# Half of the SSM input moved from the first stage to a later chunk, with the vector engine's order and the slots of the side jobs moved to match

## The chip, the core and the metric

The kernel runs on one core of one Trainium2 chip. The metric is the time of one execution on the device in microseconds (us), the median of three runs. TensorE is called PE here, VectorE DVE, ScalarE ACT, GpSimd POOL and SyncE SP, as in the profile.

## The reference, cut to what matters

One layer over 256 tokens of width 2048, all in 32-bit floats:

```
mod  = silu(c) @ W_ada + b_ada                 # shift1, scale1, gate1, shift2, scale2, gate2
h    = rms_norm(x) * (1 + scale1) + shift1
p    = h @ W_in                                # conv value, conv gate, ssm input u, ssm gate: 1024 columns each
yc   = swish(layer_norm(causal_conv31(value * sigmoid(gate))))
ys   = gelu(diagonal_ssm(u) + u * d) * sigmoid(ssm_gate)
x    = x + gate1 * (concat(rms_norm(yc), rms_norm(ys)) @ W_out)
x    = x + gate2 * top2_of_32_experts(rms_norm(x) * (1 + scale2) + shift2)
out  = rms_norm(x)
```

The state-space model (SSM) is worked in eight quads of 128 channels: per quad PE makes the drive from one tile of u, DVE rotates it, scans it in two halves and rotates it back, and PE reads the states out into one tile of the SSM's output.

## The kernel before, in words

**Weights.** All large weights pass through `ring`, 12 buffers of 1 MB. SP starts one load per unit in a fixed order; the load of unit n waits until PE has consumed unit n - 12. There are 40 units in stage A, 88 in stage B, 16 in stage C (the output projection), and then 48 for each of eight rounds of four experts (L484).

**Stage A** (`A_LIST`, L67): for each quarter b of the 2048 channels, four units of the scale columns of W_ada, four of the shift columns, and, between the units of quarter b + 1, two units of W_in for u (all 1024 columns, two rows of channels each). A column unit is eight matmuls (L524). After four of them PE signals, ACT copies the row (`column_copy`, L1110), PE turns it into columns (`columns`, L535), DVE adds the bias, and after a shift DVE scales hT (L1566), on which the u units of that quarter wait (L563). In the same stage DVE makes the phases of the sine and cosine tables (L1595 to L1600) behind its `columns(3)`; ACT turns them into tables (L1148, L1153, L1157), and its `column_copy(4)` stands in its queue behind L1148, `column_copy(5)` behind L1153. The last u unit releases the eight tiles of u.

**Stage B** is 24 steps. Step g is 2 or 3 `ada` units (eight matmuls each, L707, for gate1, shift2, scale2 and gate2, 16 units a part, all into PSUM bank 2), `side(2g)`, one unit of a chunk of W_in (32 matmuls, L722; four units make a chunk of 512 columns), and `side(2g + 1)`. `CHUNKS` lists the chunks. The lists `DRIVE_AT`, `READ_AT` and `SUM_AT` put the side jobs into slots: the drive of a quad (L755), the read-out of a quad (L769, L772, then ACT's gelu, L1200), and three sums over channels (L740) for the conv's layer norm and RMS norm. PE runs its program in order, so a side job that is not ready stops it. Between two parts of the ada units stands a chain: PE's first unit of part i + 1 waits for ACT's `ada_copy(i)` (L1181, out of bank 2 into `modrow`), and `ada_copy(i)` waits until POOL's `columns(i - 1)` (L1387 to L1401) has emptied `modrow`. In before, the last units of the parts fall into steps 5, 11, 17 and 23.

**POOL** works, in its order: the skip diagonals of the quads (L1380, each behind the read-out of the quad before it), `columns(0)` to `columns(3)`, and the two products value * gate (`z_tiles`, L1410). Its order in before is diagonals 0 to 3, columns(0), diagonal 4, z_tiles(1), diagonal 5, columns(1), diagonal 6, z_tiles(0), diagonal 7, columns(2), columns(3).

**DVE** works quads 0 to 4, the upper half of the conv (`convolve(1, 0)`: 124 instructions, L1664 and L1668, back to back), quads 5 and 6, the lower half of the conv, the tile sum (L1677), then centring, the sum of squares, scaling, the first half of quad 7, the last sum of squares, `norm_conv` (L1697, L1699), and the second half of quad 7. The tables, the conv and other tiles share memory: conv lies on the cosines of quads 0 to 3.

**ACT**, in step 19, waits for scale2 (`parts_ready` 3) and stores scale2 and shift2 to memory, and in step 20 waits for that store and loads them back as rows; the copy of the first sum (L1205) stands behind this.

**Stage C**: output unit 0 waits for the last chunk and for `norm_conv`; then read-out 7, units 1 and 2, the SSM's sum of squares, and so on. Behind the 16 units come the router and the experts.

Of the kernel before, what the change touches and what calls it, by code (L numbers as in the profile page):

```python
# [61 lines left out]
A_UNITS, B_UNITS, C_UNITS, D_UNITS = 40, 88, 16, 48  # L62
# [17 lines left out]


def ada_in_step(g):

    return 3 if g % 3 else 2
# [6 lines left out]
DRIVE_AT = [0, 1, 4, 7, 10, 13, 27, 29]  # L91
READ_AT = [3, 7, 9, 13, 15, 29, 32, 49]
SUM_AT = [42, 44, 47]
# [18 lines left out]
def stored_before(chunk, b):  # L112

    return 2 + b if chunk == 0 else 4 + 2 * (chunk - 1) + b + 1
# [7 lines left out]
def trunk(nc, a, out):  # L122

    ctx = ExitStack()
    with ctx:
# [308 lines left out]
        def _(sp):  # L434
# [10 lines left out]
            for n, (kind, b, i) in enumerate(A_LIST):  # L445
                unit = ring[:, n % RING, :]
                if kind == "u":
                    k = 4 * b + 2 * i
                    start(n, unit.rearrange("p (k n) -> p k n", k=2), w_in[:, k:k + 2, 2 * CH:3 * CH])
# [54 lines left out]
        def _(pe):  # L504
# [46 lines left out]
            def u_unit(n, b, i):  # L551

                if b == 0 and i == 0:
# [4 lines left out]
                def tiles(pair, kk):  # L558
                    k = 4 * b + 2 * i + kk
                    pe.wait_ge(h_ready, k + 1)  # L560
                    for j in range(2):
                        o = kk * CH + (2 * pair + j) * P
# [4 lines left out]
                if b == 3 and i == 1:  # L567
                    for pair in range(4):
                        for kk in range(2):
                            last = tiles(pair, kk)  # L570
                        if pair < 3:
# [3 lines left out]
                else:  # L575
                    for kk in range(2):
                        for pair in range(4):
# [59 lines left out]
            def a_unit(n):  # L637
                kind, b, i = A_LIST[n]
                if kind == "u":
                    u_unit(n, b, i)  # L640
# [23 lines left out]
            for n in range(8, 14):  # L664
                a_unit(n)
            turn_blocks(0)
            turn_blocks(1)
            columns(2)
            a_unit(14)
            a_unit(15)  # L670
            turn_blocks(2)
            turn_blocks(3)
            a_unit(16)
            a_unit(17)
# [3 lines left out]
            for n in range(18, 21):  # L678
                a_unit(n)
            turn_blocks(6)  # L680
            for n in range(21, 24):
# [3 lines left out]
            for n in range(24, 28):  # L685
                a_unit(n)
            columns(5)
            for n in range(28, 34):
                a_unit(n)
            columns(6)  # L690
            for n in range(34, 38):
                a_unit(n)
            columns(7)
            a_unit(38)
            a_unit(39)
# [18 lines left out]
            def chunk_unit(n, it, u):  # L714

                s = arrived(n)
                for kk in range(4):
                    k = 4 * u + kk
                    for j in range(4):
                        if k == 0 and j % 2 == 0:  # L720
# [21 lines left out]
            def side(slot):  # L742
                for job, q in side_jobs(slot):
                    if job == "drive":

                        pe.wait_ge(chunk_stored, q // 2 + 1)
# [11 lines left out]
                    elif job == "read":  # L758
                        if q:
                            pe.wait_ge(side_stored, q)  # L760
                        else:
                            pe.wait_ge(chunk_stored, 4)
# [277 lines left out]
        def _(act):  # L1040
# [127 lines left out]
            for pair in range(4):  # L1168
# [14 lines left out]
            def keep_chunk(it):  # L1183

                act.wait_ge(chunk_done, 4 + it + 1)
                _c0, kind, tile = CHUNKS[it]
                func, dst = {"gate": (ACT.Sigmoid, zT[:, :, PAD:]), "value": (ACT.Copy, vals), "out_gate": (ACT.Sigmoid, sgT)}[kind]
# [32 lines left out]
            for g in range(STEPS_B):  # L1220
# [17 lines left out]
            side(49)  # L1238
# [115 lines left out]
        def _(pool):  # L1354
# [51 lines left out]
            def z_tiles(h):  # L1406

                pool.wait_ge(chunk_stored, 4 + 2 * (VALUE_0, VALUE_1)[h] + 2)
# [71 lines left out]
        def _(dve):  # L1480
# [127 lines left out]
            def quad(q, middle=None):  # L1608
# [36 lines left out]
                if middle:  # L1645
                    middle()

# [326 lines left out]
```

## Time and profile before

| what | value |
|---|---|
| median of three runs | 1560.77 us (1560.55 to 1563.14) |
| the profiled execution's own time | 1561.5 us |
| its span | 1559.8 us |
| mean granted PE clock | 0.975 |
| busy share of the span, PE / DVE / ACT / POOL | 92% / 33% / 10% / 8% |
| end of the first stage's last u unit | 147.2 us |
| start of output unit 0 | 438.0 us |

Times in the profile are us from the span's start. A timeline row merges like instructions that follow one another: start, time from the first start to the last end, engine, line, operation, tiles, count, and in brackets the engine's idle time before the row and what ended it.

### The profile page before, as it was taken

To read this page: it belongs to the slowest core of one execution; us is meant where nothing else is said; L and a number is where in the kernel's file an instruction comes from. 1 tells how busy PE (TensorE), PEld (TensorE's weight loads), DVE (VectorE), ACT (ScalarE), POOL (GpSimd) and SP (SyncE) were. 2 spreads that over 40 slices of the span, in tenths; PEclk is the share of its full clock that TensorE was granted. 3 is DMA by queue.
4 is the path that set the end of the run, shared out by engine and by line. 5 is a ranking of instruction groups with operands and counts; after the bars stand their busy time and mean duration, and the time that the engine had idled before them with its cause. 6 is when DMAs were issued, how large, how long until landed. Compare 5 with 4: busy or idle time off the path is not lost.

```text
span 1559.8 us, 18926 instructions
## 1 busy us (share of the span) xinstructions
PE 1440.0 (92%) x7448; PEld 665.8 (43%) x7448; DVE 519.8 (33%) x934; ACT 160.0 (10%) x254; POOL 131.0 (8%) x112
## 2 busy tenths in 40 slices
PE   5999999989779979999999999999999999999967
PEld 2667666656534434343343343343343343343322
DVE  4231999999651230121121121111111111111105
ACT  3040100100310211010010010010010010000001
POOL 1000011539000017000000000000000000000000
PEclk9799999999989989999999999999999999999989
DMA  9999988979646437999999999999999999999991
GB/s 319 388 391 409 356 307 311 389 284 389 219 168 236 145 126 289 422 421 421 421 422 422 421 423 422 422 422 422 422 421 422 421 423 421 423 421 422 422 420 75
DMA packets 108961, 565.47 MB, mean 363 GB/s; under 512 B 10632, under 2 KB 10816, under 8 KB 50608
## 3 DMA queue, kind: packets, MB, share of 16 engines
q1 hardware_dynamic: 105984, 559.98, 89.2%
q10 hardware_dynamic: 2928, 4.81, 1.0%
q8 instruction: 34, 0.56, 0.1%
q14 instruction: 15, 0.12, 0.0%
HBM read 562.62 MB, written 2.13 MB: 362 GB/s over the span
## 4 chain that ended last, share of the span: by engine, by line
PE 62%; DVE 13%; DMA 11%; issue 7%; PEld 4%; PEldq 1%; SPq 1%; ACT 1%; POOL 0%; DVEq 0%; ACTq 0%
PE ps L918 20%; PE ps L952 15%; DMA ring<-in_exp_w_down 10%; PE ps L890 7%; PE ps L972 6%; PE ps L722 3%; DVE arena L1668 3%; PE ps L563 3%; DVE arena L1635 2%; PEld ps L811 2%; PE ps L508 2%; DMA ring<-in_w_ada 1%; PE ps L707 1%; PE ps L524 1%; DVE arena L1623 1%
## 5 line engine op out<-in xcount | busy, mean ns | idle before, releaser
L918 PE MATMUL ps<-ring,arena 128*64 128x512 f32 x2048 | 458.4, 594 | 11.3 <-DMA ring<-in_exp_w_up 7.7
L918 PEld LDWEIGHTS ps<-ring,arena 128*64 128x64 f32 x2048 | 154.6, 137 | 287.9 <-issue 285.9
L952 PE MATMUL ps<-ring,arena 128*64 128x512 f32 x1024 | 242.9, 600 | 26.8 <-issue 13.9
L722 PE MATMUL ps<-arena,ring 128*128 128x256 f32 x768 | 174.5, 386 | 0.4
L722 PEld LDWEIGHTS ps<-arena,ring 128*128 128x128 f32 x768 | 146.0, 192 | 36.8 <-issue 17.2
L952 PEld LDWEIGHTS ps<-ring,arena 128*64 128x64 f32 x1024 | 72.2, 137 | 167.0 <-issue 158.7
L1875 DVE TENSOR_TENSOR arena<-arena,ps 128x512 f32<-128x512 f32 x72 | 49.6, 689 | 277.5 <-PE ps L972 262.8
L890 PE MATMUL ps<-arena 128*64 128x256 f32 x1024 | 123.7, 386 | 6.4 <-issue 3.8
L811 PE MATMUL ps<-ring,arena 128*128 128x512 f32 x256 | 114.1, 605 | 5.8 <-DVE arena L1699 5.7
L1849 DVE TENSOR_SCALAR arena<-ps,mod 128x256 f32<-128x256 f32 x64 | 34.8, 544 | 228.4 <-PE ps L890 228.4
L972 PE MATMUL ps<-arena 128*64 128x512 f32 x448 | 106.5, 595 | 2.9 <-issue 1.9
L890 PEld LDWEIGHTS ps<-arena 128*64 128x64 f32 x1024 | 73.2, 138 | 69.9 <-issue 42.1
L1668 DVE SCALAR_TENSOR_TENSOR arena<-arena 128x256 f32<-128x256 f32 x240 | 95.2, 480 | 0.0
L811 PEld LDWEIGHTS ps<-ring,arena 128*128 128x128 f32 x256 | 49.0, 194 | 67.2 <-issue 66.9
L1863 DVE TENSOR_TENSOR arena<-arena,ps 128x512 f32<-128x512 f32 x16 | 11.0, 688 | 178.2 <-PEq L924 177.0
L1380 POOL TENSOR_SCALAR skip<-ident,vT 128x128 f32<-128x128 f32 x8 | 50.9, 6361 | 215.4 <-PE ps L772 212.9
L1856 DVE TENSOR_TENSOR arena<-ps,arena 128x512 f32<-128x512 f32 x64 | 44.3, 692 | 66.4 <-PEq L958 66.4
L1302 ACT ACTIVATE arena<-ps,mod 128x256 f32<-128x256 f32 x64 | 36.1, 564 | 279.0 <-PE ps L890 279.0
L972 PEld LDWEIGHTS ps<-arena 128*64 128x64 f32 x448 | 32.0, 137 | 70.1 <-issue 70.1
L707 PE MATMUL ps<-ring,ccol 128*32 128x512 f32 x512 | 59.8, 596 | 0.7 <-issue 0.5
L563 PE MATMUL ps<-arena,ring 128*128 128x256 f32 x256 | 57.0, 381 | 1.7 <-issue 0.9
L524 PE MATMUL ps<-ring,ccol 128*32 128x512 f32 x256 | 39.0, 729 | 18.8 <-DMA ring<-in_w_ada 18.8
(262 smaller groups left out, 747.1 us busy)
## 6 DMA issues: line engine op xcount, KB each, us to landing
ring<-in_exp_w_gate SPq DMA_DIRECT2D x128, 1024.0 KB, 19.7
ring<-in_exp_w_up SPq DMA_DIRECT2D x128, 1024.0 KB, 18.7
ring<-in_exp_w_down SPq DMA_DIRECT2D x128, 1024.0 KB, 22.5
ring<-in_w_ada SPq DMA_DIRECT2D x96, 1024.0 KB, 9.0
ring<-in_w_in SPq DMA_DIRECT2D x32, 1024.0 KB, 11.9
ring<-in_w_out SPq DMA_DIRECT2D x16, 1024.0 KB, 11.6
arena<-in_x SPq DMA_DIRECT2D x2, 1024.0 KB, 7.0
arena<-in_x SPq DMA_DIRECT2D x1, 2048.0 KB, 10.4
```

Of the source, the lines that this page charges most:

```text
L524: last = mm(ps[32 * j:32 * j + 32, bank, :], ccol[:, k:k + 1].to_broadcast([P, 32]), ring[:, s, j * N:(j + 1) * N], start=(i == 0), stop=( ...
L563: last = mm(ps[:, U_BANKS[pair], j * T:(j + 1) * T], ring[:, s, o:o + P], hT[:, k, :], start=(k == 0 and j == 0), stop=(k == KD - 1), skip ...
L707: last = mm(ps[32 * j:32 * j + 32, 2, :], ccol[:, k:k + 1].to_broadcast([P, 32]), ring[:, s, j * N:(j + 1) * N], start=(k == 0), stop=(k = ...
L722: last = mm(ps[:, j // 2, (j % 2) * T:(j % 2 + 1) * T], ring[:, s, kk * N + j * P:kk * N + (j + 1) * P], hT[:, k, :], start=(k == 0 and j ...
L811: last = mm(ps[:, OUT_BANKS[c][t], :], src[:, k0 + kk, t * P:(t + 1) * P], ring[:, s, kk * N:(kk + 1) * N], start=first, stop=end, skip_gr ...
L890: last = mm(ps[half, 6 + k % 2, 0:T], x1p[:, t, k, half], pick[:, t, :], start=(t == 0), stop=(t == 1), skip_group_check=True)
L918: last = mm(ps[64 * x:64 * x + 64, stage, :], xT[:, k, slot:slot + SLOTS], ring[:, s, kk * N:(kk + 1) * N], start=(k == 0), stop=(k == KD ...
L952: last = mm(ps[half, 2 + n, :], hidT[pr][:, u, half], ring[:, (m + x) % RING, n * N:(n + 1) * N], start=(u == 0), stop=(u == 3), skip_grou ...
L972: last = mm(ps[64 * x:64 * x + 64, 6 + t, :], wpickT[:, pr, t * P + 64 * x:t * P + 64 * x + 64], yexp[pr][:, n, :], start=(pr == 0), stop= ...
L1380: gp_.tensor_scalar(skip[:, :], ident[:, :], vT[:, 4, q:q + 1], None, ALU.mult).then_inc(skip_ready, 1)
L1668: ins = V.scalar_tensor_tensor(conv[:, c, :], z, cwT[:, c, j:j + 1], conv[:, c, :], ALU.mult, ALU.add)
L1875: V.tensor_tensor(acc[:, t, cc], acc[:, t, cc], ps[:, bank, :], ALU.add).then_inc(added, 1)
```

## The change

Half of u (512 of its 1024 columns, quads 0 to 3) stays in stage A, in four units of four rows of channels each; the other half becomes the third chunk of stage B. Stage A has 36 units, stage B 92 in 28 steps, with one ada unit in even and two in odd steps up to step 19, and then 4, 4, 4, 4, 4, 5, 5, 4. Only the first tile pair (two banks) of u is released at the end of stage A. DVE's order becomes quads 0 to 3, upper conv, quads 4 to 6, lower conv, the whole of the conv's norm, quad 7. POOL's z_tiles(1) stands ahead of diagonal 4 and columns(0), and z_tiles(0) ahead of columns(1). The store and reload of scale2 and shift2 move from ACT to SP, before stage C's units 8 and 9.

```diff
-A_UNITS, B_UNITS, C_UNITS, D_UNITS = 40, 88, 16, 48
+A_UNITS, B_UNITS, C_UNITS, D_UNITS = 36, 92, 16, 48
 for _b in range(3):
-    A_LIST += [("scale", _b + 1, 0), ("scale", _b + 1, 1), ("u", _b, 0), ("scale", _b + 1, 2), ("scale", _b + 1, 3),
-               ("u", _b, 1)] + [("shift", _b + 1, i) for i in range(4)]
-A_LIST += [("u", 3, 0), ("u", 3, 1)]
+    A_LIST += [("scale", _b + 1, 0), ("scale", _b + 1, 1), ("u", _b, 0), ("scale", _b + 1, 2), ("scale", _b + 1, 3)]
+    A_LIST += [("shift", _b + 1, i) for i in range(4)]
+A_LIST += [("u", 3, 0)]
-U_BANKS = [2, 0, 1, 3]
+U_BANKS = [2, 3]
-CHUNKS = [(1536, "gate", 4), (512, "value", 0), (1024, "gate", 0), (0, "value", 0), (3072, "out_gate", 0), (3584, "out_gate", 4)]
-VALUE_1, VALUE_0 = 1, 3
+CHUNKS = [(1536, "gate", 4), (512, "value", 0), (2560, "u", 4), (1024, "gate", 0), (0, "value", 0),
+          (3072, "out_gate", 0), (3584, "out_gate", 4)]
+VALUE_1, U_1, VALUE_0 = 1, 2, 4
-STEPS_B = 24
+STEPS_B = 28
 def ada_in_step(g):
-    return 3 if g % 3 else 2
+    if g < 20:
+        return 2 if g % 2 else 1
+    return 5 if g in (25, 26) else 4
-DRIVE_AT = [0, 1, 4, 7, 10, 13, 27, 29]
-READ_AT = [3, 7, 9, 13, 15, 29, 32, 49]
-SUM_AT = [42, 44, 47]
+DRIVE_AT = [0, 3, 6, 9, 25, 28, 31, 35]
+READ_AT = [5, 9, 13, 17, 31, 35, 38, 58]
+SUM_AT = [49, 51, 54]
...
                     sp.wait_ge(side_done, QUADS)
                     sp.dma_start(x1, a["x"][0].rearrange("(t p) d -> p t d", p=P)).then_inc(x_again, 16)
+                    sp.wait_ge(parts_ready, 3)
+                    for i, part in enumerate((4, 3)):
+                        sp.dma_start(col(ab_dram[i]), mod[:, part, :]).then_inc(ab_stored, 16)
+                if m == 9:
+                    sp.wait_ge(ab_stored, 32)
+                    sp.wait_ge(z_ready, 2)
+                    sp.dma_start(ab_rows, ab_dram.rearrange("i (k p) -> (i k) p", p=P)).then_inc(ab_landed, 16)
...
             out_units([0])
-            side(49)
             out_units([1, 2])
+            side(58)
+            out_units([3, 4])
             channel_sum(3)
-            out_units([3, 4])
+            out_units([5, 6, 7])
             pe.wait_ge(ab_landed, 16)
             tr(ps[:, 6, 0:2 * KD], ab_rows, 2 * KD).then_inc(ab_turned, 1)
-            out_units(range(5, 10))
+            out_units([8, 9])
...
-                if g == 9:
+                if g == 14:
                     act.wait_ge(parts_ready, 1)
                     act.dma_start(col(gate_dram[0]), mod[:, 2, :]).then_inc(gate_stored, 16)
-                if g == 19:
-                    act.wait_ge(parts_ready, 3)
-                    for i, part in enumerate((4, 3)):
-                        act.dma_start(col(ab_dram[i]), mod[:, part, :]).then_inc(ab_stored, 16)
-                if g == 20:
-                    act.wait_ge(ab_stored, 32)
-                    act.wait_ge(z_ready, 2)
-                    act.dma_start(ab_rows, ab_dram.rearrange("i (k p) -> (i k) p", p=P)).then_inc(ab_landed, 16)
...
             for q in range(4):
                 diagonal(q)
+            z_tiles(1)
+            diagonal(4)
             columns(0)
-            diagonal(4)
-            z_tiles(1)
             diagonal(5)
-            columns(1)
             diagonal(6)
+            diagonal(7)
             z_tiles(0)
             pool.wait_ge(z_ready, 2)
             gp_.memset(mean_w, 1.0 / CH).then_inc(sum_consts, 1)
-            diagonal(7)
+            columns(1)
             columns(2)
             columns(3)
...
-            for q in range(5):
+            for q in range(4):
                 quad(q)
             convolve(1, 0)
-            quad(5)
-            quad(6)
+            for q in range(4, 7):
+                quad(q)
             convolve(0, 1)
...
             scale_conv()
-
-            def finish_conv():
-                add_squares(2)
-                norm_conv()
-
-            quad(7, finish_conv)
+            add_squares(2)
+            norm_conv()
+            quad(7)
```

## Rows read from the trace of the kernel before

**Rows 1.** Windows of two stretches; columns: us, PE, PEld, DVE, ACT, POOL busy, PEclk, DMA share, GB/s

```profile
40.00:60.00 20.00, 19.71 (x111) 12.80 (x111) 7.88 (x15) 0.59 (x1) 0.00 (x0) 0.65 1.06 387
...
1000.00:1100.00 100.00, 96.18 (x502) 36.51 (x500) 15.92 (x25) 5.70 (x10) 0.00 (x0) 1.00 1.01 422
```

**Rows 2.** Timeline of PE in stage A

```profile
33.49 1.93 PE L524 MATMUL ps<-ring,ccol 128*32 128x512 f32 x8 [0.44 <-DMA ring<-in_w_ada]
...
101.43 0.95 PE L535 MATMUL ps<-arena,modrow 128*128 128x1 f32 x8
...
125.95 0.95 PE L535 MATMUL ps<-arena,modrow 128*128 128x1 f32 x8
...
133.14 14.05 PE L563 MATMUL ps<-arena,ring 128*128 128x256 f32 x64 [0.87 <-DVE arena L1566]
```

**Rows 3.** Timeline of DVE and ACT in stage A, the tables

```profile
83.58 4.42 DVE L1595 TENSOR_TENSOR arena<-arena 128x4096 f32<-128x4096 f32 x1
...
95.48 3.62 ACT L1148 ACTIVATE arena<-arena 128x4096 f32<-128x4096 f32 x1 [1.51 <-DVE rot L1600]
...
99.24 0.59 ACT L1110 COPY modrow<-ps 128x512 f32<-128x512 f32 x1
```

**Rows 4.** Timeline of PE in stage B, quiet steps

```profile
251.45 7.17 PE L722 MATMUL ps<-arena,ring 128*128 128x256 f32 x32
...
299.34 7.17 PE L722 MATMUL ps<-arena,ring 128*128 128x256 f32 x32
...
306.45 1.15 PE L755 MATMUL ps<-arena 32*128 32x256 f32 x16
...
307.52 2.78 PE L707 MATMUL ps<-ring,ccol 128*32 128x512 f32 x24
...
317.77 1.93 PE L772 MATMUL ps<-arena 128*32 128x256 f32 x32
```

**Rows 5.** Timeline of DVE: conv halves, starts of quads 5 and 6, tile sum

```profile
249.84 47.59 DVE L1668 SCALAR_TENSOR_TENSOR arena<-arena 128x256 f32<-128x256 f32 x120
...
297.35 2.28 DVE L1622 TENSOR_TENSOR arena<-ps,arena 128x2048 f32<-128x2048 f32 x1
...
316.16 2.29 DVE L1622 TENSOR_TENSOR arena<-ps,arena 128x2048 f32<-128x2048 f32 x1
...
338.15 47.60 DVE L1668 SCALAR_TENSOR_TENSOR arena<-arena 128x256 f32<-128x256 f32 x120
...
385.85 3.79 DVE L1677 TENSOR_REDUCE arena<-arena 128x256 f32<-128x2048 f32 x1
```

**Rows 6.** Timeline of POOL in stage B

```profile
280.89 17.46 POOL L1387 TENSOR_TENSOR modrow<-modrow,own 128x512 f32<-128x512 f32 x1 [31.16 <-ACT modrow L1181]
...
332.28 2.39 POOL L1410 TENSOR_TENSOR arena<-arena 128x1024 f32<-128x1024 f32 x1 [11.84 <-ACT arena L1194]
...
341.23 45.00 POOL L1380 TENSOR_SCALAR skip<-ident,vT 128x128 f32<-128x128 f32 x1 [6.29 <-PE ps L772]
...
386.19 1.06 POOL L1387 TENSOR_TENSOR modrow<-modrow,own 128x512 f32<-128x512 f32 x1
...
389.71 0.22 POOL L1396 TENSOR_TENSOR mod<-mod,bada 128x16 f32<-128x16 f32 x1
```

**Rows 7.** Timeline of PE around the end of stage B

```profile
406.15 1.19 PE L740 MATMUL ps<-arena 128*128 128x256 f32 x2 [6.12 <-issue]
...
407.14 9.62 PE L722 MATMUL ps<-arena,ring 128*128 128x256 f32 x32
...
437.99 9.59 PE L811 MATMUL ps<-ring,arena 128*128 128x512 f32 x16 [5.73 <-DVE arena L1699]
```

**Rows 8.** Timeline of ACT and SP, the first sum, the swish, the experts' second loads

```profile
397.79 0.37 ACT L1205 COPY arena<-ps 128x256 f32<-128x256 f32 x1 [19.65 <-DMA scale_shift_scratch<-mod]
...
412.00 4.04 ACT L1215 ACTIVATE arena<-arena,vT 128x256 f32<-128x256 f32 x8 [2.85 <-DVE arena L1693]
...
536.34 63.53 SPq L484 DMA_DIRECT2D ring<-in_exp_w_up  x8
```

More of the change, by code:

```diff
@@ L112, in stored_before @@
 def stored_before(chunk, b):
-    return 2 + b if chunk == 0 else 4 + 2 * (chunk - 1) + b + 1
+    return 2 + 2 * (chunk - 1) + b + 1 if chunk else 0
 JOB_ORDER = [(stage, pr, u, x) for pr in range(2) for stage in range(2) for u in range(4) for x in range(2)] + \
@@ L447, in _ @@
                 if kind == "u":
-                    k = 4 * b + 2 * i
-                    start(n, unit.rearrange("p (k n) -> p k n", k=2), w_in[:, k:k + 2, 2 * CH:3 * CH])
+                    start(n, unit.rearrange("p (k n) -> p k n", k=4), w_in[:, 4 * b:4 * b + 4, 2 * CH:2 * CH + N])
                 else:
@@ L548, in turn_x, with u_unit @@
                 last.then_inc(x_turned, 1)
-            def u_unit(n, b, i):
-                if b == 0 and i == 0:
+            def u_unit(n, b):
+                if b == 0:
                     pe.wait_ge(x_even, 4)
@@ L558, in tiles @@
                 def tiles(pair, kk):
-                    k = 4 * b + 2 * i + kk
+                    k = 4 * b + kk
                     pe.wait_ge(h_ready, k + 1)
                     for j in range(2):
-                        o = kk * CH + (2 * pair + j) * P
+                        o = kk * N + (2 * pair + j) * P
                         last = mm(ps[:, U_BANKS[pair], j * T:(j + 1) * T], ring[:, s, o:o + P], hT[:, k, :],
@@ L565, in tiles @@
                     return last
-                if b == 3 and i == 1:
-                    for pair in range(4):
-                        for kk in range(2):
+                if b == 3:
+                    for pair in range(2):
+                        for kk in range(4):
                             last = tiles(pair, kk)
-                        if pair < 3:
+                        if pair == 0:
                             last.then_inc(chunk_done, 1)
@@ L575, in u_unit @@
                 else:
-                    for kk in range(2):
-                        for pair in range(4):
+                    for kk in range(4):
+                        for pair in range(2):
                             last = tiles(pair, kk)
@@ L639, in a_unit @@
                 if kind == "u":
-                    u_unit(n, b, i)
+                    u_unit(n, b)
                 else:
@@ L663, in _ @@
             columns(1)
-            for n in range(8, 14):
+            for n in range(8, 13):
                 a_unit(n)
@@ L668, in _ @@
             columns(2)
+            a_unit(13)
             a_unit(14)
-            a_unit(15)
             turn_blocks(2)
             turn_blocks(3)
+            a_unit(15)
             a_unit(16)
-            a_unit(17)
             turn_blocks(4)
@@ L677, in _ @@
             turn_blocks(5)
-            for n in range(18, 21):
+            for n in range(17, 20):
                 a_unit(n)
             turn_blocks(6)
-            for n in range(21, 24):
+            for n in range(20, 22):
                 a_unit(n)
@@ L684, in _ @@
             columns(4)
-            for n in range(24, 28):
+            for n in range(22, 26):
                 a_unit(n)
             columns(5)
-            for n in range(28, 34):
+            for n in range(26, 31):
                 a_unit(n)
             columns(6)
-            for n in range(34, 38):
+            for n in range(31, 35):
                 a_unit(n)
             columns(7)
-            a_unit(38)
-            a_unit(39)
+            a_unit(35)
             def ada_unit(n, i, k):
@@ L719, in chunk_unit @@
                     for j in range(4):
-                        if k == 0 and j % 2 == 0:
+                        if it and k == 0 and j % 2 == 0:
                             pe.wait_ge(chunk_stored, stored_before(it, j // 2))
@@ L744, in side @@
                     if job == "drive":
-                        pe.wait_ge(chunk_stored, q // 2 + 1)
+                        pe.wait_ge(chunk_stored, q // 2 + 1 if q < 4 else 2 + 2 * U_1 + q // 2 - 1)
                         if q:
@@ L761, in side @@
                         else:
-                            pe.wait_ge(chunk_stored, 4)
+                            pe.wait_ge(chunk_stored, 2)
                         if sums_before(slot):
@@ L1167, in _ @@
             column_copy(7)
-            for pair in range(4):
+            for pair in range(2):
                 act.wait_ge(chunk_done, pair + 1)
@@ L1183, in keep_chunk @@
             def keep_chunk(it):
-                act.wait_ge(chunk_done, 4 + it + 1)
+                act.wait_ge(chunk_done, 2 + it + 1)
                 _c0, kind, tile = CHUNKS[it]
-                func, dst = {"gate": (ACT.Sigmoid, zT[:, :, PAD:]), "value": (ACT.Copy, vals), "out_gate": (ACT.Sigmoid, sgT)}[kind]
+                func, dst = {"u": (ACT.Copy, uT), "gate": (ACT.Sigmoid, zT[:, :, PAD:]), "value": (ACT.Copy, vals), "out_gate": (ACT.Sigmoid, sgT)}[kind]
                 if it == VALUE_0:
@@ L1406, in z_tiles @@
             def z_tiles(h):
-                pool.wait_ge(chunk_stored, 4 + 2 * (VALUE_0, VALUE_1)[h] + 2)
+                pool.wait_ge(chunk_stored, 2 + 2 * (VALUE_0, VALUE_1)[h] + 2)
                 z = zT[:, 4 * h:4 * h + 4, PAD:]
@@ L1607, in _, with quad @@
             dve.wait_ge(tables_ready, 2)
-            def quad(q, middle=None):
+            def quad(q):
                 b = q % 2
```

4 lines of the change are left out of this document (1 added, 3 removed).

## The prediction

> **What bounds the kernel now.** I read the windows first. In the expert rounds DMA is busy all the time at 422 GB/s [rows 1], and the last ring loads ahead of them are only released by the first expert matmuls [rows 8]. So the rounds end a fixed time after they begin, and they begin a fixed time after output unit 0, behind which PE has its queue full. What the change moves is the start of output unit 0, 438.0 in the trace [rows 7]. Then the timelines. Stage A is two lines at once: DMA is full (share 1.06, 387 GB/s, so 2.71 us for a unit of 1.049 MB [rows 1]) and yet PE waits for no load after 33.5 us [rows 2], since its own work is slower than the loads. It ends with the u units at 147.2 [rows 2]. Stage B is PE-bound while DVE runs beside it. At its end DVE comes last: PE waits 6.1 us for the second sum, whose chunk then takes 9.6 us where a warm one takes 7.2, and 5.7 us for the conv's norm, whose unit 0 takes 9.6 [rows 4, 7].
>
> An effect of less than 0.2% (3.1 us) can't be told from none here.
>
> **Stage A.** Four u units leave. Two take 14.05 us [rows 2], so PE has 28.1 us less to do. Not all of it comes off:
> - The tables. Two of the four stood ahead of `columns(4)`, so PE comes to it at 101.4 - 14.1 = 87.3. ACT's copy for it ended at 99.83 [rows 3], behind the sine and DVE's phases, which start behind `columns(3)` (83.58), with one u unit fewer ahead: 99.8 - 7.0 = 92.8. PE now waits 5.5 us where it waited for nothing.
> - The clock. After 6.1 us without work the next chunk took 2.5 us longer [rows 7, 4]; I take 2.5 us for this wait.
> - `columns(6)` was covered by a u unit ahead of it (125.95 [rows 2]); now the copy (0.59 [rows 3]) and two hand-overs show: 0.8 us.
> - DMA. The last u unit is number 35; unit 5 landed at 33.5 [rows 2], so it lands at 33.5 + 30 x 2.71 = 114.8, ahead of its use at about 120. No cost, with 5 us of cover.
> Stage B thus starts at 147.2 - 28.1 + 5.5 + 2.5 + 0.8 = 127.9.
>
> **Stage B, PE's work.** From 251.45 to 299.34 PE did five steps with 13 ada units [rows 4]. An ada unit is 2.78 / 3 less the overlap, 0.905; so a chunk unit with its hand-overs is (47.9 - 11.8) / 5 = 7.22. A drive is 1.07 (306.45 to 307.52), a read-out 2.4 (0.5 and 1.93 [rows 4]). After the change: 28 x 7.22 = 202.2, 64 x 0.905 = 57.9, 8 drives 8.6, 7 read-outs 16.8, three sums 1.5: 287.0 us.
>
> **The new waits.** Drive 5 waits until DVE has read drive 4, which is behind the upper conv: the value chunk ends with step 7, 80 us into the stage, and 1.1 us of copies, 3 of POOL, 49 of conv and 4.6 of reading (two instructions of 2.28 [rows 5]) follow, while PE comes to drive 5 after 135 us: 3 us. Read-out 6 and the first ada unit of part 2: 0.4 and 0.8 us.
>
> The large one is at step 24. Twice a POOL instruction that met the conv was held to its end: the product of `columns(1)` started at 280.89 and ended at 298.35, where alone it takes 1.06; diagonal 7 lasted from 341.23 to 386.23 [rows 5, 6]. Before, neither mattered. Now `columns(1)` stands directly behind z_tiles(0), whose end is what starts the lower conv. Its first instruction may slip in; the rest waits for the conv's end. ACT's copy of part 2 needs it, and part 3's first ada unit, the third of step 24, needs the copy. With t the end of step 19's chunk: copies 1.1, product 2.4, hand-overs 0.3, conv 48.9 [rows 5, 6] give t + 52.7; POOL's remaining 2.7 of its 3.7 us (386.19 to 389.93) and the copy make it t + 56.1. PE gets there after four chunks, 18 ada units and the 0.8: t + 46.0. PE stands still for 10.1 us, and then pays 2.5 for the clock.
>
> The Trainium skill (SBUF — State Buffer, Who interferes with whom) says that a DVE instruction with two SBUF inputs and a GpSimd instruction that reads SBUF exclude each other, the lock being held for one instruction. The trace agrees on the exclusion and not on the length: a conv instruction lasts 0.4 us, and POOL waited 45.
>
> **DVE after the lower conv.** Its end is t + 52.7, the tile sum 3.8 [rows 5] more; the first sum's slot is behind step 24's chunk, at t + 56.1 + 1.8 + 7.2 = t + 65.1. So PE is late by 8.6 us. From there DVE and ACT need 9 us to the second sum (8.4 from 397.79 to 406.15, and the first copy [rows 7, 8]) against PE's 11.8 (five ada units and a chunk); then 15 us to the third (4.7 from the second sum's end at 407.3 to the swish at 412.0, swish 4.0 [rows 7, 8], square 1.8, half of the 4096-column activation's 3.62 [rows 3], tile sum 3.8 [rows 5], hand-overs) against 15.3; then 5.7 for the norm [rows 7] against 7.2 of the last chunk and 1.3 for its copies, which PE does wait for. PE is the bound with little to spare, and ACT's wait for the reload of scale2, which held the first sum's copy (19.65 us idle behind it [rows 8]), is gone from the path. It moves to SP, ahead of C's units 8 and 9: issued with read-out 7, needed 35 us later; nothing. Quad 7 (18.8 us, 297.35 to 316.16 [rows 5]) runs behind the norm, beside output units 0 to 2; its read-out comes 21 us after unit 0's start. Nothing. The order of the SSM's tail behind units 3 and 4 has 7 us of cover (unit 5).
>
> DMA in steps 20 to 27: 42 units in about 100 us at 2.5 to 2.7 us each, 105 to 113, of which twelve (30 us) are in the ring at the start. No cost; if the ring were empty, 10 us.
>
> **The sum.** Output unit 0 starts at 127.9 + 287.0 + 3 + 0.4 + 0.8 + 10.1 + 2.5 + 1.3 = 433.0, which is 5.0 before 438.0; and it starts after 1.3 us of idleness, not 5.7, so that its 2.6 us for the clock go too. 7.6 us off the profiled execution's 1561.5 is 1553.9, and that execution stands 0.7 above the median: 1553.
>
> Bounds of the unseen costs: the clock's price after the two new waits, from 0 to 5 us each; the wait for `columns(1)`, from 0 (POOL gets in between conv instructions) to 12 (the first instruction is held too); the 3 us of drive 5, from 0 to 5.
>
> **The rivals.**
> 1. POOL isn't held. By the skill's rule as it stands, the lock ends with each 0.4 us instruction, `columns(1)` would be done some 10 us after its start, long before step 24. Worked out from rows: the 10.1, the 2.5 and their knock-on go, 0.7 for the first sum comes, and the end is 12 us earlier: 1541. Against it are two rows of 17 and 45 us that end exactly with a conv. 0.12.
> 2. DVE's chain misses its slots. The cover at the three sums is 8.6, 3 and 0.3 us. If scans or sums run longer, as beside POOL's work they can, PE waits at the third sum, goes cold and pays as before: 4 + 2.5 us, 1560. 0.10.
> 3. Slower: PE's clock falls in stage A and stays low. At 40 to 60 us the granted clock was 0.65 of full, and eight matmuls took 1.93 us at such a time where eight in stage B take 0.93 [rows 1, 2, 4]. With two u units fewer ahead of them, the column units 22 to 35 meet four waits in a row. All fourteen at the low clock cost 14 less the 2.5 counted, the two u units 2.5 each: 16.5 us, B starts at 144, and the end is 1553 + 16.5 = 1569. It decides from a B start at about 136 on (no gain) and 139 (slower). For it: the waits are new. Against: from 80 us on the trace has small waits and a full clock. 0.08.
> The forecast itself: 0.70.
>
> **Numbers.** The forecast's own range is 1548 to 1558. The range given takes in most of rival 2 and some of rival 1: 1543 to 1561; what is left out is most of rival 1 and rival 3, 0.18. Faster than 1557.7: 0.69 of the forecast and rival 1, with a little of rival 2, 0.82. Same: the rest of rival 2 and a little of rival 3, 0.09. Slower: 0.09.
>
> **What would show it.** Stage B's first matmul near 128; a wait of 5 us before `columns(4)`; POOL's second or third instruction of `columns(1)` lasting some 47 us and ending with the lower conv; PE idle 10 us in step 24 behind ACT's copy; the first sum without a wait; output unit 0 near 433 at 7 us; equal times from there on. The prediction is wrong if the B start is past 133, if `columns(1)` ends before the conv, or if PE waits for sums 2 or 3.

## The result, and the profile after

The changed kernel takes 1542.93 us (1540.21 to 1544.64, four runs) against 1560.66 (1559.72 to 1563.14, four runs of the kernel before on the same chip); the ratio is 0.9882, 95% interval 0.9863 to 0.9902. It is 17.7 us faster. The forecast was 7.8 us (1553, with a range of 1543 to 1561), so the sign was right and the size too small by more than half; the measured median lies at the lower edge of the range, 0.1 us outside it. The profiled execution took 1544.6 us, its span is 1542.9; before they were 1561.5 and 1559.8.

The first fence is the timeline of PE in the changed kernel, at the places where the prediction had a term. `columns` is now L544, a column unit L533, an ada unit L715, a chunk unit L730, the sums L748, the output units L819.

```profile
93.20 1.86 PE L544 MATMUL ps<-arena,modrow 128*128 128x1 f32 x8 [5.37 <-ACT modrow L1119]
...
94.99 5.42 PE L533 MATMUL ps<-ring,ccol 128*32 128x512 f32 x32
...
101.17 1.05 PE L544 MATMUL ps<-arena,modrow 128*128 128x1 f32 x8 [0.76 <-ACT modrow L1119]
...
113.79 1.05 PE L544 MATMUL ps<-arena,modrow 128*128 128x1 f32 x8 [0.75 <-ACT modrow L1119]
...
121.08 7.14 PE L572 MATMUL ps<-arena,ring 128*128 128x256 f32 x32 [0.86 <-DVE arena L1567]
...
128.48 1.06 PE L715 MATMUL ps<-ring,ccol 128*32 128x512 f32 x8 [0.26 <-issue]
...
264.97 1.15 PE L763 MATMUL ps<-arena 32*128 32x256 f32 x16 [1.14 <-DVE arena L1624]
...
316.84 0.67 PE L777 MATMUL ps<-arena,skip 128*128 128x256 f32 x2 [0.41 <-issue]
...
329.26 1.92 PE L715 MATMUL ps<-ring,ccol 128*32 128x512 f32 x16 [0.75 <-ACT modrow L1190]
...
373.08 1.92 PE L715 MATMUL ps<-ring,ccol 128*32 128x512 f32 x16 [0.75 <-ACT modrow L1190]
...
384.35 0.67 PE L748 MATMUL ps<-arena 128*128 128x256 f32 x2 [2.23 <-issue]
...
384.94 6.19 PE L715 MATMUL ps<-ring,ccol 128*32 128x512 f32 x40
...
423.02 20.84 PE L819 MATMUL ps<-ring,arena 128*128 128x512 f32 x48 [1.27 <-ACT arena L1203]
```

These answer to [rows 2, 4, 7]. `columns(4)` waits 5.4 us and then takes 1.86 instead of 0.95, the four units behind it 5.4 instead of 3.6: the granted clock between 93 and 101 us was 0.65, and 1.00 in the same work before (101 to 106 us). Stage B starts at 128.5 (147.4 before). Drive 5 waits 1.1 us, read-out 6 0.4, the first ada unit of part 2 0.75. Then the row that matters: the first ada unit of part 3, at 373.08, waits 0.75 us and not 10.1. PE therefore comes to the first sum too early and waits 2.2 us there, after which five ada units take 6.2 us instead of 4.5, at a granted clock of 0.76 (384 to 391 us). Output unit 0 starts at 423.0 (438.0 before), 1.3 us behind the last chunk, and three output units take 20.8 us.

The timelines of POOL and DVE around the lower conv (L1411 is the product, L1388 to L1397 `columns(1)`, L1662 and L1666 the conv) answer to [rows 5, 6]:

```profile
218.58 42.19 POOL L1381 TENSOR_SCALAR skip<-ident,vT 128x128 f32<-128x128 f32 x1 [7.28 <-PE ps L780]
...
327.73 2.18 POOL L1411 TENSOR_TENSOR arena<-arena 128x1024 f32<-128x1024 f32 x1 [7.63 <-ACT arena L1203]
...
330.14 1.21 POOL L1388 TENSOR_TENSOR modrow<-modrow,own 128x512 f32<-128x512 f32 x1
...
331.43 2.05 POOL L1391 TENSOR_TENSOR modrow<-modrow 128x256 f32<-128x256 f32 x4
...
333.92 0.32 POOL L1397 TENSOR_TENSOR mod<-mod,bada 128x16 f32<-128x16 f32 x1
...
373.11 8.29 POOL L1388 TENSOR_TENSOR modrow<-modrow,own 128x512 f32<-128x512 f32 x1 [38.88 <-ACT modrow L1190]
```

```profile
330.02 2.82 DVE L1662 TENSOR_SCALAR arena<-arena 128x256 f32<-128x256 f32 x4 [13.28 <-POOL arena L1411]
...
332.76 47.73 DVE L1666 SCALAR_TENSOR_TENSOR arena<-arena 128x256 f32<-128x256 f32 x120
...
380.59 3.66 DVE L1675 TENSOR_REDUCE arena<-arena 128x256 f32<-128x2048 f32 x1
```

A conv half is four tensor_scalar instructions and then 120 scalar_tensor_tensor instructions that overlap: each waits for the one four before it, starts 0.396 us after its predecessor and lasts 0.48. `columns(1)` came directly behind POOL's own work, 0.12 us after the first tensor_scalar, and was over at 334.2, 46 us before the conv's end. It wasn't held: its seven instructions took 4.1 us in all, against 3.7 in [rows 6]. DVE paid too, with 2.82 us for the four tensor_scalar instructions instead of the 1.38 to 1.46 that they take where `columns(1)` isn't beside them. Three of the seven POOL instructions began among the four tensor_scalar ones; the other four, all of at most 64 columns, among the first overlapping ones. But diagonal 4, which met the upper conv 5.9 us after its scalar_tensor_tensor instructions had begun, lasted 42 us, and the first instruction of `columns(2)`, at 373.11, lasted 8.3 us, past the end of the lower conv at 380.5.

Behind output unit 0 the times are nearly the same: the first expert matmul (L927) starts at 570.95, 17.2 us earlier than its counterpart of before at 588.13, where output unit 0 was 15.0 earlier and 2.6 us of slow clock in it are gone (9.6 us for 16 matmuls before, 20.8 for 48 now). The span is 16.9 shorter.

### The profile page after: what moved, and what is told of

It reads as the page before. It is cut to its first block, busy times and chain, and to the rows that moved or that the text cites. A ratio compares the mean times of both kernels' runs of the same rounds, so it can differ in the third digit from the quotient of the medians.

```text
span 1542.9 us, 18923 instructions
## 1 busy us (share of the span) xinstructions
PE 1440.0 (93%) x7448; PEld 663.8 (43%) x7448; DVE 516.6 (33%) x934; ACT 159.7 (10%) x254; POOL 116.3 (8%) x112
## 3 DMA queue, kind: packets, MB, share of 16 engines
q1 hardware_dynamic: 108368, 560.02, 90.4%
## 4 chain that ended last, share of the span: by engine, by line
PE 55%; DVE 12%; DMA 12%; PEld 8%; issue 8%; PEldq 3%; SPq 1%; ACT 1%; POOL 0%; DVEq 0%; ACTq 0%
PE ps L927 20%; PE ps L961 15%; DMA ring<-in_exp_w_down 10%; PE ps L899 8%; PE ps L981 6%; DVE arena L1666 6%; PEld ps L730 4%; PEld ps L819 2%; PE ps L517 2%; DMA ring<-in_w_ada 1%; PE ps L819 1%; DVE arena L1636 1%; PEldq L823 1%; PEldq L735 1%; PE ps L533 1%
## 5 line engine op out<-in xcount | busy, mean ns | idle before, releaser
L927 PE MATMUL ps<-ring,arena 128*64 128x512 f32 x2048 | 458.3, 594 | 11.7 <-DMA ring<-in_exp_w_up 8.1
L927 PEld LDWEIGHTS ps<-ring,arena 128*64 128x64 f32 x2048 | 154.7, 137 | 288.0 <-issue 286.2
L730 PE MATMUL ps<-arena,ring 128*128 128x256 f32 x896 | 200.8, 383 | 0.1
L730 PEld LDWEIGHTS ps<-arena,ring 128*128 128x128 f32 x896 | 168.4, 190 | 42.2 <-issue 20.9
L819 PE MATMUL ps<-ring,arena 128*128 128x512 f32 x256 | 111.4, 594 | 1.3 <-ACT arena L1203 1.3
L1666 DVE SCALAR_TENSOR_TENSOR arena<-arena 128x256 f32<-128x256 f32 x240 | 95.3, 480 | 0.0
L819 PEld LDWEIGHTS ps<-ring,arena 128*128 128x128 f32 x256 | 48.3, 190 | 60.3 <-issue 60.0
L715 PE MATMUL ps<-ring,ccol 128*32 128x512 f32 x512 | 62.8, 612 | 2.3 <-ACT modrow L1190 1.5
L533 PE MATMUL ps<-ring,ccol 128*32 128x512 f32 x256 | 40.5, 756 | 19.3 <-DMA ring<-in_w_ada 19.3
L1314 ACT COPY arena<-ps 128x512 f32<-128x512 f32 x16 | 9.4, 585 | 380.3 <-PE ps L517 380.3
```

Of the source, the lines that this page charges most:

```text
L533: last = mm(ps[32 * j:32 * j + 32, bank, :], ccol[:, k:k + 1].to_broadcast([P, 32]), ring[:, s, j * N:(j + 1) * N], start=(i == 0), stop=( ...
L715: last = mm(ps[32 * j:32 * j + 32, 2, :], ccol[:, k:k + 1].to_broadcast([P, 32]), ring[:, s, j * N:(j + 1) * N], start=(k == 0), stop=(k = ...
L730: last = mm(ps[:, j // 2, (j % 2) * T:(j % 2 + 1) * T], ring[:, s, kk * N + j * P:kk * N + (j + 1) * P], hT[:, k, :], start=(k == 0 and j ...
L819: last = mm(ps[:, OUT_BANKS[c][t], :], src[:, k0 + kk, t * P:(t + 1) * P], ring[:, s, kk * N:(kk + 1) * N], start=first, stop=end, skip_gr ...
L927: last = mm(ps[64 * x:64 * x + 64, stage, :], xT[:, k, slot:slot + SLOTS], ring[:, s, kk * N:(kk + 1) * N], start=(k == 0), stop=(k == KD ...
L1666: ins = V.scalar_tensor_tensor(conv[:, c, :], z, cwT[:, c, j:j + 1], conv[:, c, :], ALU.mult, ALU.add)
```

## The experiments

**Why `columns(1)` wasn't held.** Four kernels. The first, `late8`, holds it back until the lower conv has done eight instructions:

```diff
+            pool.wait_ge(conv_step, 4 * TAPS + 8)
             columns(1)
             columns(2)
```

> The changed kernel, with columns(1) on POOL held back until the second conv half has done eight instructions. Arrival theory (POOL is shut out only if it comes while conv instructions already follow one another without a gap; in the changed kernel it was at work when the conv began): the first POOL instruction of columns(1) starts near 334 and ends with the conv at about 381, PE waits about 13 us before its 49th ada unit in step 24, and the time is 1543 + 11 = about 1554. Rival (the POOL instructions of columns(1) are never held by the conv, and the long rows of the kernel before have another cause): columns(1) is over by about 339, no wait in step 24, 1543.

Measured: 1551.51 us (1549.78 to 1552.54), ratio 0.9945 (0.9929 to 0.9962): 8.6 us slower than the changed kernel. POOL's timeline and PE's:

```profile
330.62 46.77 POOL L1388 TENSOR_TENSOR modrow<-modrow,own 128x512 f32<-128x512 f32 x1 [2.89 <-DVE arena L1667]
...
377.47 1.99 POOL L1391 TENSOR_TENSOR modrow<-modrow 128x256 f32<-128x256 f32 x4
```

```profile
380.48 3.64 PE L715 MATMUL ps<-ring,ccol 128*32 128x512 f32 x16 [10.57 <-ACT modrow L1190]
```

The first instruction, 1.06 us alone, was held for 46.8 us to the end of the conv half (376.5), and PE waited 10.6 us in step 24. Only the moment of arrival differs from the changed kernel: these are the same POOL and DVE instructions. In `late1` the wait is for four instructions in place of eight, that is until the tensor_scalar instructions are done:

> The changed kernel, with columns(1) held back only until the four first instructions (tensor_scalar) of the second conv half are done. Arrival theory: it depends on a few tenths of a us; if POOL gets its first instruction in before the overlapping run of scalar_tensor_tensor has formed, all of columns(1) goes through in 5 us; if not, its first instruction lasts 47 us. Rival (never held): 5 us.

Measured in a single execution: 1550.98 us. POOL came at 330.94, when the first scalar_tensor_tensor had been at work for 0.18 us, and its first instruction lasted 48.3 us. It came 1.5 us after the conv's first instruction, in the changed kernel 0.12 us after it; that decides. The edge isn't sharp, though. In `b_order`, a kernel described below, a diagonal met the upper conv 0.35 us after its first scalar_tensor_tensor (at 247.43), behind 1.75 us of idleness, and wasn't held:

```profile
247.78 0.91 POOL L1381 TENSOR_SCALAR skip<-ident,vT 128x128 f32<-128x128 f32 x1 [1.75 <-PE ps L772]
```

In `b_both` the same diagonal came 1.56 us after the first one and lasted 46.5 us. Why the one got in and `late1`'s wider instruction (512 columns), which came earlier still, didn't, no run shows.

`late8_gaps` keeps the wait for eight instructions and takes the overlap out of the conv:

```diff
-                            dve.wait_ge(conv_step, done - 3)
+                            dve.wait_ge(conv_step, done if turn else done - 3)
```

> As the run before (columns(1) comes eight instructions into the conv), but each instruction of the lower conv half waits for the one before it instead of the one four before, so that there is a gap between them. Arrival theory: POOL gets in at such a gap, columns(1) is over within some 5 us of its arrival, PE has no wait of over 1 us for it; the conv half is longer, by 120 gaps of some 0.06 to 0.1 us, 7 to 12 us. Rival (what shuts POOL out is the conv's kind of instruction, not that they follow without a gap): columns(1) lasts until the conv's end again.

Measured in a single execution: 1558.84 us. POOL's and DVE's timelines:

```profile
332.61 1.06 POOL L1388 TENSOR_TENSOR modrow<-modrow,own 128x512 f32<-128x512 f32 x1 [3.39 <-DVE arena L1667]
...
333.74 2.30 POOL L1391 TENSOR_TENSOR modrow<-modrow 128x256 f32<-128x256 f32 x4
...
336.61 0.44 POOL L1397 TENSOR_TENSOR mod<-mod,bada 128x16 f32<-128x16 f32 x1
...
372.15 1.16 POOL L1388 TENSOR_TENSOR modrow<-modrow,own 128x512 f32<-128x512 f32 x1 [35.09 <-ACT modrow L1190]
```

```profile
330.48 64.89 DVE L1667 SCALAR_TENSOR_TENSOR arena<-arena 128x256 f32<-128x256 f32 x120
```

`columns(1)` arrived among the scalar_tensor_tensor instructions, as in `late8`, and was over in 4.4 us; `columns(2)` arrived 39.5 us later, behind 35 us of idleness, and went through too. Nothing was held. The conv instructions are of the same kind with the same operands; what is gone is their overlap. It costs DVE more than expected: 120 instructions take 64.9 us instead of 47.6, on average 0.144 us more for each (0.125 where POOL is idle, between 340 and 372 us), and PE waits 18 us at the first sum.

`stay` adds sixty POOL instructions directly behind `columns(1)`:

```diff
             columns(1)
+            for _ in range(60):
+                link(gp_.tensor_tensor(spare, ident[:, 0:64], ident[:, 64:128], ALU.add))
             columns(2)
```

> The changed kernel, with sixty more POOL instructions of two SBUF inputs and 64 columns directly behind columns(1), on a tile that nothing reads: some 0.3 us each with 0.08 between. Arrival theory: once at work, POOL stays in turn with DVE; all sixty are done within 20 to 35 us, none lasts over 1 us, and the conv is longer by a few us. Rival (each POOL instruction draws anew, and in the changed kernel it was luck): one of the sixty is held until the conv's end at about 381 and the rest come after it.

Measured in a single execution: 1547.8 us. POOL's and DVE's timelines:

```profile
332.98 27.68 POOL L1427 TENSOR_TENSOR arena<-ident 128x64 f32<-128x64 f32 x60
...
371.96 12.07 POOL L1389 TENSOR_TENSOR modrow<-modrow,own 128x512 f32<-128x512 f32 x1 [11.30 <-ACT modrow L1191]
```

```profile
331.54 51.57 DVE L1669 SCALAR_TENSOR_TENSOR arena<-arena 128x256 f32<-128x256 f32 x120
```

All sixty went through in 27.7 us, in the middle of the conv, 0.46 us each, as against the 0.3 and 0.08 us that I had put down. The conv's 120 instructions took 51.6 us, 4.0 more. The two engines took strict turns: in those 27.7 us DVE started sixty instructions too, one every 0.46 us instead of 0.396. POOL then stopped for want of work, and when `columns(2)` came at 371.96 its first instruction lasted 12 us, to the conv's end. So in one and the same conv a POOL that was already at work went on, and a POOL that arrived was shut out. One rival is left untested: everything that POOL began among overlapping instructions and got through had at most 64 columns, except the diagonal of 128 in `b_order`, and everything held had 128 or 512. No run sends a wide instruction in turn or lets a narrow one arrive, so `stay` doesn't tell turn from width. For the prediction's term it doesn't matter: `late8` and `late1` hold back the same first instruction that the changed kernel let through.

**Which part of the change brought the time.** Three kernels put parts of the change into the kernel before, with its stage A, its 24 steps and its slots. `b_ab` moves the store and reload of scale2 and shift2 from ACT to SP; `b_order` has

```diff
-            quad(7, finish_conv)
+            add_squares(2)
+            norm_conv()
+            quad(7)
...
             out_units([0])
-            side(49)
             out_units([1, 2])
+            side(49)
```

with the fourth sum behind output units 3 and 4 and the turning of the reloaded rows behind unit 7 (in `b_ab` too); `b_both` has both.

> The kernel before with the store and reload of scale2 and shift2 moved from ACT to SP, nothing else. Theory of the end: the first sum's copy on ACT, at 397.8 in the kernel before, follows the sum at once at about 390, and everything behind it is 7 us earlier: 1554. Theory of PE's queue: under 3 us.

> The kernel before with quad 7 whole behind the conv's norm and its read-out behind output units 1 and 2, nothing else. Theory of the end: the third sum no longer waits for the first half of quad 7 (15.5 us), but for the swish and its square instead (ends 418.0), so the norm is done some 5 to 8 us earlier: 1554 to 1556. Theory of PE's queue: under 3 us.

> The kernel before (all of u in stage A, 24 steps, the old slots) with two parts of the change: quad 7 whole behind the conv's norm, its read-out behind output units 1 and 2, and the store and reload of scale2 and shift2 on SP. Theory of the end (what counted in the kernel before was the chain on DVE and ACT behind the second conv half, and these two parts shorten it): output unit 0 starts 11 to 12 us earlier, near 426, the time is 1561 - 12 = 1549, and the split of u gives the other 6. Theory of PE's queue (the gain is PE's work and idleness in stages A and B, brought by the split): 1561 to 1557, the split gives 14 or more.

Measured: `b_ab` 1555.80 us, ratio 0.9968 (0.9955 to 0.9980); `b_order` 1557.28, 0.9979 (0.9969 to 0.9988); `b_both` 1548.08, 0.9917 (0.9901 to 0.9934). So the two small edits together bring 12.6 us of the 17.7, where alone they bring 4.9 and 3.4. PE's timeline shows what each leaves behind (L747 and L740 are the sums, L818 and L811 the output units):

```profile
387.89 0.67 PE L747 MATMUL ps<-arena 128*128 128x256 f32 x2 [0.91 <-issue]
...
422.35 1.19 PE L747 MATMUL ps<-arena 128*128 128x256 f32 x2 [6.61 <-DVE arena L1676]
...
429.28 9.48 PE L818 MATMUL ps<-ring,arena 128*128 128x512 f32 x16 [5.74 <-DVE arena L1698]
```

```profile
387.56 1.19 PE L740 MATMUL ps<-arena 128*128 128x256 f32 x2 [4.56 <-issue]
...
403.47 1.19 PE L740 MATMUL ps<-arena 128*128 128x256 f32 x2 [3.34 <-issue]
...
424.29 0.67 PE L740 MATMUL ps<-arena 128*128 128x256 f32 x2 [0.37 <-issue]
...
432.10 18.34 PE L811 MATMUL ps<-ring,arena 128*128 128x512 f32 x37 [7.14 <-DVE arena L1700]
```

In `b_ab` the early part of the chain is quick (the first sum's copy at 388.6 follows the sum at once), but PE then waits 6.6 us for the third sum behind the first half of quad 7. In `b_order` that wait is gone (0.4), but the first sums are late as before, since ACT's copy (395.1) still stands behind the reload. Measured from the first scalar_tensor_tensor of the lower conv (338.15 before [rows 5], 332.76 in the changed kernel) to output unit 0, free of the executions' differing starts, the way is 99.8 us before, 93.0 in `b_ab` (from 336.3), 96.0 in `b_order` (from 336.1), 90.4 in `b_both` and 90.3 in the changed kernel. DVE's and PE's timelines of `b_both`:

```profile
341.62 47.63 DVE L1668 SCALAR_TENSOR_TENSOR arena<-arena 128x256 f32<-128x256 f32 x120
```

```profile
432.00 18.35 PE L818 MATMUL ps<-ring,arena 128*128 128x512 f32 x37 [7.14 <-DVE arena L1699]
```

So the two edits shorten this way by 6.8 and 3.8 us alone and 9.4 together, and they make it as short as in the changed kernel; the rest of the change, with the split of u, only lets it begin earlier. That the median of `b_both` is 12.6 us lower and not 9.4 stays open: its interval reaches from 10.3 to 15.5 us. Its profiled execution (1554.9 us, mean granted clock 0.972) was the longest of the five; the other four took 1546.1 to 1548.2 us at 0.979, so that it is a poor witness for the median. It lost 3.1 us before the way begins: its last two u units took 17.1 us instead of 14.05, at a granted clock of 0.82 (133 to 151 us).

The other way round, two kernels undo one part each of the changed kernel:

> The changed kernel with the first half of quad 7 put back between scaling and the conv's last sum, and its read-out back behind output unit 0. Theory of the end: the third sum comes 7 us later, PE waits 7 us for it and pays 2 to 3 for the clock, 1543 + 8 = 1551. Theory of PE's queue: 1543 to 1545.

> The changed kernel with the store and reload of scale2 and shift2 back on ACT, in step 24 ahead of the first sum's copy. Theory of the end: scale2 is ready at 384.7 (columns(2) on POOL is held until the conv's end), the round trip through memory takes 7 us, so the first sum's copy comes at 391.5 instead of 385.1; PE waits some 3 us for the second sum and some for the third: 1543 + 4 to 8. Rival (PE's work alone is the bound, the chain of sums has cover): under 2 us.

Measured: with the first half of quad 7 back in the middle 1552.26 us, ratio 0.9952 (0.9935 to 0.9969), 9.3 slower than the changed kernel; with the round trip on ACT 1550.60, 0.9931 (0.9914 to 0.9948), 7.7 slower. PE's timeline of each:

```profile
418.42 1.19 PE L748 MATMUL ps<-arena 128*128 128x256 f32 x2 [8.32 <-DVE arena L1678]
```

```profile
382.90 0.67 PE L741 MATMUL ps<-arena 128*128 128x256 f32 x2 [2.22 <-issue]
...
401.09 1.19 PE L741 MATMUL ps<-arena 128*128 128x256 f32 x2 [5.99 <-issue]
...
428.27 20.84 PE L812 MATMUL ps<-ring,arena 128*128 128x512 f32 x48 [1.27 <-ACT arena L1196]
```

The waits are where the theory of the end has them: 8.3 us at the third sum in the one, 6.0 at the second in the other. In the changed kernel PE waits 0.4 us for the third sum, and DVE's `norm_conv` ends at 421.3, 1.7 us before output unit 0: the chain on ACT and DVE and PE's work end within 2 us of each other. Both additions to the chain lengthened the whole.

**Towards a faster version.** `copies_first` takes the wait out of stage A, with ACT's `column_copy(4)`, `keep_read(7)` and `column_copy(5)` ahead of the sine:

```diff
+            column_copy(4)
+            keep_read(7)
+            column_copy(5)
             act.wait_ge(phase_ready, 1)
             A(sinT, cosT, ACT.Sin, scale=TWO_PI_DOWN).then_inc(table_sin, 1)
             A(rot128[:, 1, :], rot128[:, 0, :], ACT.Sin, scale=TWO_PI_DOWN).then_inc(table_sin, 1)
-            column_copy(4)
-            keep_read(7)
...
-            column_copy(5)
```

> The changed kernel with ACT's column_copy(4) and column_copy(5) ahead of the sine of the tables instead of behind the sine and the absolute value. If the wait of 5.4 us ahead of columns(4) is what the first stage gave back, it goes, with 1.8 us for the clock and 0.8 ahead of columns(5); the last u unit's load lands near 115 and its use would come at 113 to 115, so the whole is 5 to 7 us: stage B starts near 122, 1543 - 6 = 1537. Rival (the loads are the bound of the first stage already): stage B starts at 127 or later, 1542.

Measured: 1541.26 us (1540.08 to 1543.09), ratio 0.9873 (0.9855 to 0.9891), 1.7 us less than the changed kernel where 6 were expected, and within the spread of the runs: whether it is faster than the changed kernel isn't shown. PE's timeline:

```profile
85.98 1.05 PE L544 MATMUL ps<-arena,modrow 128*128 128x1 f32 x8
...
94.73 1.06 PE L533 MATMUL ps<-ring,ccol 128*32 128x512 f32 x8 [1.34 <-DMA ring<-in_w_ada]
...
97.44 10.05 PE L572 MATMUL ps<-arena,ring 128*128 128x256 f32 x32 [1.65 <-DMA ring<-in_w_in]
...
117.42 8.60 PE L572 MATMUL ps<-arena,ring 128*128 128x256 f32 x32 [0.86 <-DVE arena L1567]
...
126.28 1.06 PE L715 MATMUL ps<-ring,ccol 128*32 128x512 f32 x8 [0.26 <-issue]
```

The wait before `columns(4)` is gone (85.98). In its place PE waits for the loads, 1.3 and 1.7 us, and the clock falls: the u unit at 97.44 takes 10.05 us (granted clock 0.71 between 97 and 108 us), the last one 8.6 (0.83 between 117 and 127), where one at full clock takes 7.17. Stage B starts at 126.3, 2.2 us earlier and not 6. Both theories had a part: the ACT wait was real, and once it is gone the loads are the next thing that PE waits for.

`sixth` moves ada units between steps:

```diff
-    return 5 if g in (25, 26) else 4
+    return {24: 6, 25: 3, 26: 5}.get(g, 4)
```

> The changed kernel with 6, 3 and 5 instead of 4, 5 and 5 ada units in steps 24, 25 and 26, so that PE reaches the first sum 1.8 us later. If the wait of 2.2 us at that sum and the slow clock behind it (5 ada units in 6.2 us instead of 4.5) are real costs: the wait falls to about 0.4, the five units run at full clock, 1543 - 3 = 1540. Rival (DVE's chain behind the sum is the bound and PE's wait costs nothing): no difference.

Measured: 1540.25 us (1539.21 to 1542.02), ratio 0.9865 (0.9849 to 0.9882). The wait at the first sum is 0.56 us, output unit 0 starts at 419.6. That is the size expected, but the runs overlap with those of the changed kernel.

> Both of the two edits above together, with everything of the change: 1543 - 6 - 3 = 1534, between 1532 and 1539. If each only moves PE's idleness into the next wait: 1540 or more.

Measured for both edits together: 1538.95 us (1538.15 to 1541.19), ratio 0.9862 (0.9844 to 0.9880), output unit 0 at 417.6. It is the lowest median of the study, 4.0 us under the changed kernel and not the 9 expected, at the upper end of the range given; its interval overlaps with the changed kernel's, so that it beats the kernel before is shown, and that it beats the changed kernel is likely only.

## Why the prediction was wrong in its size

**The step that failed** is the large new wait: "Its first instruction may slip in; the rest waits for the conv's end." Not only the first instruction slipped in but all seven of `columns(1)`. The 10.1 us in step 24 were 0.75, and the 2.5 us of the clock behind it didn't come. In their place came 2.2 us at the first sum and 1.7 of slow clock behind that, which the same sum of the prediction had covered with the delay. That makes 7.9 us of the 10.0 by which output unit 0 came earlier than forecast (423.0 against 433.0). The mechanism exists: `late8` differs only in when POOL arrives and costs 8.6 us, with the wait of 10.6 us where the prediction had it. What was wrong was the rule that I drew from [rows 6]. Both long rows began well inside a conv half, behind idle stretches of 31.16 and 6.29 us that stand in the same rows. They say what happens to a POOL that arrives there, and I used them for one that was at work before the overlapping instructions had begun. The case was there as rival 1, with 1541 us, but for another reason (the lock ending with each instruction, whoever comes) and at 0.12. The Trainium skill (SBUF — State Buffer, Who interferes with whom) says that whoever issues first gets the shared pair for the whole instruction, a sentence on DVE's two-port modes, and that issue order decides who blocks. The changed kernel and `late8` agree that the order decides (0.75 us of wait in step 24 against 10.6). On the length they differ from the page: with overlapping DVE instructions the hold lasted up to 48.3 us, where one conv instruction lasts 0.48, and with a gap between them (`late8_gaps`) there was none: POOL's 512 columns took 1.06 and 1.16 us. What happens inside the engines between two overlapping instructions, no run shows.

**Drive 5** was put at 3 us and took 1.14. The upper conv began at 211.4, where the working had 212.0, since POOL's product took 2.2 us and not 3, and PE came 0.9 us later than worked out. With these 1.9 us, 9.8 of the 10.0 are found; what else there was nearly cancels: stage B began 0.6 late, the third sum waited 0.4, and the work counted as 287.0 took 1.1 less.

**Stage A** held term by term: the wait before `columns(4)` 5.5 (5.4 measured), the clock 2.5 (1.8 in the units and 0.8 in the columns), `columns(6)` 0.8 (0.75). The wait of 0.76 before `columns(5)` isn't new, it was 0.86 before. Stage B was forecast to start at 127.9 and started at 128.5; 0.26 of the 0.6 is the hand-over behind the last u unit, which the working, counting from that unit's end at 147.2, left out. I gave the loads 5 us of cover at the last unit alone and left out those in between. In the changed kernel PE waits for none of them, but in `copies_first` it waits for units 27 and 28, the latter landing at 97.4 where 33.5 + 23 x 2.71 is 95.8.

**PE's work in stage B** held. The start at 128.5, the 287.0 us and the waits as measured (1.1, 0.4, 0.75, 0.75, 2.2, 1.7 of slow clock, 0.4 at the third sum, 1.3) give 424.1; output unit 0 started at 423.0. That the times of before carry over to PE's queue was the strong part of the prediction.

**The chain behind the lower conv** was right in its parts. Second and third sums came with 0 and 0.4 us of wait, where the cover was put at 3 and 0.3, so rival 2 didn't occur; it was near. Rival 3 (the clock falling in stage A and staying low) didn't occur either: after the 5.4 us at `columns(4)` the granted clock was 1.00 again from 101 us on. In `copies_first` its milder form is seen (0.71 and 0.83 in two u units).

**What the ledger hid.** The prediction added up PE's queue to an absolute time and gave no part of the change a price. Of the reordered quad 7 and of the store and reload on SP it says only that they cost nothing, and that ACT's old wait is gone from the path. The runs on the kernel before show that these two edits bring 12.6 of the 17.7 us there: they are what shortens the other chain far enough for PE's work to be the bound, and without either of them the changed kernel loses 9.3 or 7.7 us. The rest of the change (the split of u with its steps and slots, and the other orders of DVE and POOL, which no run separates) brings the other 5 or so (1548.1 to 1542.9, two medians whose intervals just touch).

## What to carry to other kernels

Where two engines share something, the trace's long rows must be read with the idle time in front of them: here whether POOL was held depended on when it came, and a chain of small instructions begun just before the other engine's long run went through. When a change moves the bound from one chain to another, price each part on both chains; a part with no cost on the one may carry most of the gain on the other. And a wait taken away in a stage that is also full of loads gives back only down to the next load: 2.2 us of the 6 expected in `copies_first`.

## What the runs showed of the hardware that was not expected

- A POOL instruction of 128 or 512 columns with SBUF inputs that arrives during 120 overlapping scalar_tensor_tensor instructions of DVE was held to their end (42.2, 46.8 and 48.3 us for instructions that take 0.6 to 1.1 alone), once even when it came 0.18 us after the first. The one exception came 0.35 us after the first and took 0.91 us (`b_order`).
- POOL instructions of 64 columns already following one another took turns with the same DVE instructions, one for one: sixty of them in 27.7 us, with DVE slowed by 4.0 us in 47.6.
- With each conv instruction waiting for the one before, nothing was held, and DVE paid 0.144 us an instruction, which made the run 36% longer (64.9 us against 47.6).
